# The last mixer of a four-layer chain: gate and upper projection by halves of columns, the first attention item ahead of the main loop, keys rotated later, compressed values copied later

## The reference, cut to what matters

```python
u = h @ w_in
q, kc, vc, ks, vs, kw, vw, gt, cf = jnp.split(u, offs, axis=-1)
...
# native_sparse_attention: three softmaxes over compressed, selected and window keys
q  = apply_rope(rms_norm(q, q_norm), cos, sin)
ks = apply_rope(rms_norm(k_slc, k_norm[0]), cos, sin)
kw = apply_rope(rms_norm(k_win, k_norm[1]), cos, sin)
kc = rms_norm(compress_blocks(to_bgtd(kc_tok), cmp_pos[0], cmp_w1[0], cmp_w2[0]), k_norm[2])
vc = compress_blocks(to_bgtd(v_cmp), cmp_pos[1], cmp_w1[1], cmp_w2[1])
...
# the conformer half, on the columns cf of the projection
a, b = jnp.split(cf, 2, axis=-1)
z = a * jax.nn.sigmoid(b)
z = causal_dwconv(z, conf_dw) + conf_dw_b
z = jax.nn.silu(layer_norm_2(z, conf_ln_g, conf_ln_b))
return jnp.concatenate([o_nsa, z], axis=-1) @ w_out
```

## Time and profile before

| what | value |
|---|---|
| median of 3 runs | 2250.28 us (2248.72 to 2250.85) |
| the profiled execution, its own time | 2246.99 us |
| span of the profile | 2245.2 us |
| PE busy | 2217.0 us, 99% of the span |
| DVE, ACT, POOL busy | 1632.4, 1197.9 and 129.6 us |
| last mixer, queries' projection to conformer | about 1929 to 2036 us in the span |

### The profile page before, as it was taken

How to read it: one execution, slowest core, us unless ns; L and a number is a source line. 1 busy time by engine, 2 the same in 40 slices (tenths; PEclk the granted TensorE clock), 3 DMA queues, 4 the chain that set the end, 5 groups by cost and what they waited for, 6 DMA issues and landing times.

```text
span 2245.2 us, 34615 instructions
## 1 busy us (share of the span) xinstructions
PE 2217.0 (99%) x14127; PEld 1903.4 (85%) x14127; DVE 1632.4 (73%) x2508; ACT 1197.9 (53%) x1896; POOL 129.6 (6%) x185
## 2 busy tenths in 40 slices
PE   9999999999999999999999999999999999989999
PEld 7888899878888888888898778888888888867887
DVE  5777768868676776768668867776877678666776
ACT  5555446645555545555356544655554655556653
POOL 2100010120000000000100110000000000420000
PEclk9999999999999999999999999999999999999999
DMA  7755564445556556655554446655655656643654
GB/s 243 226 188 192 188 222 122 146 142 188 190 187 192 187 186 209 192 190 195 196 181 140 140 143 210 196 188 170 215 174 171 213 188 190 200 134 117 197 176 150
DMA packets 284207, 408.17 MB, mean 182 GB/s; under 512 B 13828, under 2 KB 171072, under 8 KB 283792
## 3 DMA queue, kind: packets, MB, share of 16 engines
q1 hardware_dynamic: 276096, 380.84, 52.9%
q0 software_dynamic: 7808, 25.04, 3.8%
q10 hardware_dynamic: 144, 0.07, 0.0%
HBM read 403.98 MB, written 1.91 MB: 181 GB/s over the span
## 4 chain that ended last, share of the span: by engine, by line
PE 91%; DVE 5%; ACT 2%; DMA 1%; issue 1%; POOL 0%; SPq 0%; DVEq 0%; ACTq 0%
PE PS L575 24%; PE PS L506 13%; PE PS L513 12%; PE PS L507 12%; PE PS L574 11%; PE PS L472 3%; PE PS L473 2%; PE PS L474 2%; PE PS L577 2%; PE PS L558 1%; PE PS L556 1%; PE PS L557 1%; PE PS L492 1%; DVE WL L1391 1%; DVE QX L1698 1%; ACT WH L1007 1%
## 5 line engine op out<-in xcount | busy, mean ns | idle before, releaser
L1391 DVE TENSOR_TENSOR WL<-RW,WH 128x1024 fp32r<-128x1024 f32 (+2 forms) x678 | 806.6, 1223 | 160.4 <-ACT WH L1007 156.1
L575 PE MATMUL PS<-XT,WH 128*128 128x512 f32 x2368 | 808.0, 394 | 0.0
L1007 ACT ACTIVATE WH<-RW 128x1024 fp32r<-128x1024 f32 (+2 forms) x678 | 680.5, 1042 | 200.2 <-DMA RW<-in_w_in 40.2
L574 PE MATMUL PS<-XT,WL 128*128 128x256 f32 x2072 | 580.8, 280 | 0.0
L575 PEld LDWEIGHTS PS<-XT,WH 128*128 128x128 f32 x2368 | 425.1, 188 | 76.0
L574 PEld LDWEIGHTS PS<-XT,WL 128*128 128x128 f32 x2072 | 389.8, 188 | 13.4
L506 PE MATMUL PS<-WH,XT 128*128 128x512 f32 (+2 forms) x592 | 229.1, 391 | 1.4 <-DVE WL L1391 0.8
L507 PE MATMUL PS<-WL,XT 128*128 128x512 f32 (+2 forms) x592 | 221.4, 378 | 0.0
L506 PE MATMUL PS<-WH,HTH 128*128 128x512 f32 x488 | 192.7, 395 | 0.0
L507 PE MATMUL PS<-WL,HTH 128*128 128x512 f32 x488 | 191.5, 392 | 0.0
L513 PE MATMUL PS<-WH,XT 128*128 128x512 f32 (+2 forms) x592 | 173.5, 379 | 0.0
(11 more groups left out here) (519 smaller groups left out, 3282.7 us busy)
## 6 DMA issues: line engine op xcount, KB each, us to landing
RW<-in_w_ff_in SPq DMA_DIRECT2D x252, 512.0 KB, 4.4
RW<-in_w_ff_out SPq DMA_DIRECT2D x128, 512.0 KB, 4.4
RW<-in_w_in SPq DMA_DIRECT2D x56, 512.0 KB, 4.6
RW<-in_w_gate SPq DMA_DIRECT2D x48, 512.0 KB, 4.4
RW<-in_ffn_gate SPq DMA_DIRECT2D x44, 512.0 KB, 4.5
RW<-in_ffn_up SPq DMA_DIRECT2D x44, 512.0 KB, 4.6
RW<-in_ffn_down SPq DMA_DIRECT2D x44, 512.0 KB, 4.5
RW<-in_w_out SPq DMA_DIRECT2D x16, 512.0 KB, 4.8
```

What stands on the lines that cost most here:

```text
L574: self.e.matmul(k.PS[:, b.n, 0:T], wl, k.XTH[:, kt, :], start=False, stop=False)
L575: ins = self.e.matmul(k.PS[:, b.n, :], wh, k.XT[:, kt, :], start=kt == 0, stop=kt == 7)
L1007: self.e.activation(u.hi_out, raw, ACT.Copy).then_inc(*self.s["hi"].up(u.n))
L1391: self.e.tensor_tensor(u.lo_out, raw, u.hi_out.bitcast(F), ALU.subtract).then_inc(*self.s["lo"].up(u.n))
```

## The change

Five things are done in `mixer_odd` and its helpers.

1. The two rotations of the keys (and the copies on POOL behind the second) no longer stand ahead of the queries' projection; the first stands behind its fourth step, the second behind its eighth. `paired` stands behind the sixth and the seventh step.
2. Instead of the whole gate, the first half of the gate and the first half of the upper part are projected there, 256 columns wide, in pieces of 256 KB and eight steps as before. The main loop projects the second halves, gate first.
3. Item 0 is begun there: its scores behind the eighth step, `odd_max`, exponentials and `odd_scale` ahead of the main loop. In all items `odd_scale` stands straight behind the exponentials.
4. The copies of the compressed values to `VCB` are a function of their own, `cmp_values`, called behind item 0's exponentials; `odd_up` for the first half, `conv_out` and `conv_shift` are called before the main loop, and `conv_weights` ahead of the keys' `features`.
5. The delays of the generators change, item 1 begins with `compressed()`, and the `later` flag is gone.

```diff
     def cmp_out(self, b):
         k = self.k
         self.wait_ge("mm", b.full)
-        self.wait_ge("odd_g", "vcb0")
-        for i in range(4):
...
         kr = k.PS[:, b.n, 0:128].rearrange("p (g d) -> p g d", g=2)
...
+    def cmp_values(self, b):
+        k = self.k
+        self.wait_ge("odd_v", "kn0")
+        self.wait_ge("odd_g", "vcb0")
+        for i in range(4):
...
-        for t in range(2):
-            e.rotate("k", t, 8, 12)
         e.windows()
...
-        beside = [e.nothing] * 6 + [lambda: paired(0), lambda: paired(1)]
+        beside = [e.nothing, e.nothing, e.nothing, lambda: rotated_keys(0), e.nothing, lambda: paired(0),
+                  lambda: paired(1), lambda: rotated_keys(1)]
...
-            e.odd_scale(I)
             yield
...
+        beside = [lambda: e.rotate("q", 0, 0, 8), lambda: e.rotate("q", 1, 0, 8), hidden, cleared, hidden_turn,
+                  lambda: features("q", 0), lambda: (compressed_rows(), gated(0, gates)), lambda: next(items[0])]
+        for c0, bks in ((1816, gates), (1304, ups)):
+            for _ in self.cols(w, c0, 2, bks, self.x):
+                beside.pop(0)()
+        raised(0, ups)
+        features("q", 1)
+        next(items[0])
+        compressed_keys()
+        next(items[0])
+        e.cmp_values(*compressed_out)
+        self.drop(*compressed_out, ("odd_a", ("vcb", 3)), ("odd_v", "kn0"))
...
-            for half in range(2):
+            for c0, end in ((1816 + 256, gated), (1304 + 256, raised)):
...
-        gens = [(1, items[0]), (1, compressed()), (2, items[1]), (2, items[2]), (3, items[3]), (3, items[4]), (3, items[5]),
+        gens = [(0, items[0]), (1, compressed()), (0, items[1]), (2, items[2]), (3, items[3]), (3, items[4]), (3, items[5]),
                 (3, items[6]), (3, items[7])]
```

More of the change, by code:

```diff
@@ L459 @@
     conv_out = conv_shift = conv_weights = conv_taps4 = conv_sum = paired = odd_q = cmp_hidden = cmp_turn = cmp_out = features = keys_double = nothing
-    cmp_norm = cmp_keys = cmp_scores = cmp_probs = cmp_probs_turn = odd_scores = odd_max = odd_scale = odd_turn = odd_out = nothing
+    cmp_norm = cmp_values = cmp_keys = cmp_scores = cmp_probs = cmp_probs_turn = odd_scores = odd_max = odd_scale = odd_turn = odd_out = nothing
     conf_turn = conf_norm = conf_back = nothing
@@ L1300, in cmp_out @@
         self.wait_ge("mm", b.full)
-        self.wait_ge("odd_g", "vcb0")
-        for i in range(4):
-            r = slice(32 * i, 32 * i + 32)
-            self.e.activation(k.VCB[r, i], k.PS[r, b.n, 128:256].rearrange("p (g d) -> p g d", g=2),
-                              ACT.Copy).then_inc(*self.s["odd_a"].up(("vcb", i)))
         kr = k.PS[:, b.n, 0:128].rearrange("p (g d) -> p g d", g=2)
@@ L1311, in cmp_out @@
         self.e.activation(ms, ms, ACT.Sqrt, bias=k.eps[1e-6], scale=1.0 / 64).then_inc(*self.s["odd_a"].up("kroot"))
+    def cmp_values(self, b):
[3 more added lines that the diff above has]
+        for i in range(4):
+            r = slice(32 * i, 32 * i + 32)
+            self.e.activation(k.VCB[r, i], k.PS[r, b.n, 128:256].rearrange("p (g d) -> p g d", g=2),
+                              ACT.Copy).then_inc(*self.s["odd_a"].up(("vcb", i)))
     def cmp_keys(self, b):
@@ L3275, in mixer_odd, with rotated_keys @@
             load_w1()
-        e.keys_double()
+        def rotated_keys(t):
+            e.rotate("k", t, 8, 12)
+            if t:
+                e.keys_double()
         def paired(n):
@@ L3297, in hidden_turn @@
             self.drop(b, ("odd_a", ("gh", 1)))
+        compressed_out = []
         def compressed_rows():
@@ L3303, in compressed_rows @@
             e.prepare(ACT.Tanh)
-            self.drop(b, ("odd_a", "ksq"), ("odd_v", "kn0"))
+            compressed_out.append(b)
         def compressed_keys():
@@ L3320, in mixer_odd @@
         e.rotate_norms("q", 0, 8)
[L3324 to L3336, removed]
-        turned, done = set(), {0: [], 1: []}
[L3339 to L3355, removed]
+        turned, done = set(), {0: [], 1: []}
         def item(n, t, hs):
-            while any(ROOM[m] == ROOM[n] and m not in turned for m in range(n)) or ROOM[n] and not later["q1"]:
+            while any(ROOM[m] == ROOM[n] and m not in turned for m in range(n)) :
                 yield
@@ L3378, in item @@
                 e.prepare(ACT.Sqrt)
+            e.odd_scale(I)
             yield
-            e.odd_scale(I)
             yield
@@ L3393, in item @@
             yield
+            if n == 0:
+                yield
+                yield
+                yield
+                yield
             b = self.bank()
@@ L3401, in item, with gated, raised, cleared @@
             done[t].append(("turn_lo", I.id))
+            yield
+        items = [item(n, t, hs) for n, (t, hs) in enumerate(
+            [(0, [0, 2]), (0, [4, 6]), (0, [1, 3]), (0, [5, 7]), (1, [0, 1]), (1, [2, 3]), (1, [4, 5]), (1, [6, 7])])]
+        gates, ups = [self.bank(), self.bank()], [self.bank(), self.bank()]
+        def gated(half, bks):
+            for j in range(2):
+                e.odd_gate(2 * half + j, bks[j])
+                self.drop(bks[j], ("odd_a", ("sg", 2 * half + j)))
+        def raised(half, bks):
+            for j in range(2):
+                e.odd_up(2 * half + j, bks[j])
+                self.drop(bks[j], ("odd_v", ("zc", 2 * half + j)))
+            e.conv_out(half)
+            e.conv_shift(half)
+        def cleared():
+            e.clear_vcb()
+            for n in range(2):
+                e.conv_weights(n)
+            features("k", 0)
+            features("k", 1)
+        beside = [lambda: e.rotate("q", 0, 0, 8), lambda: e.rotate("q", 1, 0, 8), hidden, cleared, hidden_turn,
[10 more added lines that the diff above has]
+        self.drop(*compressed_out, ("odd_a", ("vcb", 3)), ("odd_v", "kn0"))
+        def compressed():
+            bks = [self.bank(), self.bank()]
+            e.cmp_scores(bks)
+            for b in bks:
+                self.drop(b, ("odd_v", "cs"))
+            yield
+            yield
+            e.cmp_probs()
+            yield
+            yield
+            b = self.bank()
+            e.cmp_probs_turn(b)
+            self.drop(b, ("odd_a", "ptc"))
             yield
@@ L3429, in upper @@
         def upper():
-            for half in range(2):
+            for c0, end in ((1816 + 256, gated), (1304 + 256, raised)):
                 bks = [self.bank(), self.bank()]
-                for n, _ in enumerate(self.cols(w, 1304 + 256 * half, 2, bks, self.x)):
+                for n, _ in enumerate(self.cols(w, c0, 2, bks, self.x)):
                     if n == 3:
[L3435 to L3439, removed]
+                        end(1, bks)
                     yield
         y = self.out_odd(Operand(k.OTH, k.OTL, lambda kt, t: done[t] if kt < 4 else [("turn_lo", ("conf", t))]))
-        items = [item(n, t, hs) for n, (t, hs) in enumerate(
-            [(0, [0, 2]), (0, [4, 6]), (0, [1, 3]), (0, [5, 7]), (1, [0, 1]), (1, [2, 3]), (1, [4, 5]), (1, [6, 7])])]
-        gens = [(1, items[0]), (1, compressed()), (2, items[1]), (2, items[2]), (3, items[3]), (3, items[4]), (3, items[5]),
+        gens = [(0, items[0]), (1, compressed()), (0, items[1]), (2, items[2]), (3, items[3]), (3, items[4]), (3, items[5]),
                 (3, items[6]), (3, items[7])]
-        up, conv, live, tick, ticks = upper(), convolve(), [], 0, 0
+        up, conv, live, tick = upper(), convolve(), [], 0
         outs = 0
@@ L3453, in mixer_odd @@
             tick += 1
-            ticks += 1
-            if ticks == 4:
-                later["q1"] = True
             live = [g for g in live if next(g, self) is not self]
```

## The result

The changed kernel takes 2253.07 us (median of 18 runs, 2250.79 to 2255.87), the kernel before 2249.96 in as many (2246.44 to 2254.76). The ratio is 1.0016 with a 95% interval of 1.0009 to 1.0022: slower by 3.1 us in the medians, and by 2 to 5 us, 0.1 to 0.2%, by the interval. The profiled executions differ by 3.80 us (2250.79 and 2246.99).

The account below looks back on a forecast made before the run. PE, busy 2217.0 of 2245.2 us, was taken as the bound, so only its waits and clock count. Terms -0.7 - 1.4 + 1.7 + 0 + 2.2 + 0 = +1.8 on the median 2250.28 gave 2252.1 us, range 2247.5 to 2256.5.

Parts of the forecast that it names:

- Keys rotated late: Gate's first steps: rotations moved into the queries' projection remove PE's wait for WL, -0.7 us.
- Values copied behind: Ahead of L897: moving the VCB copies off ACT's chain removes PE's whole wait for the compressed keys, -1.4 us.
- Item 0's softmax: Ahead of L943: chain of 9.4 us against 4.8 of PE cover, so 4.6 us of wait where 2.16 was.
- The waits behind it: After item 0's turn: 1.0 us before L920, where 2.25 was, and 0.5 before item 1's turn.
- Clock: Behind item 0's wait: the half-clock dip comes again at the same cost, 0, ends -1.7 and +1.7 us.
- Loop: Main loop: Z's wait of 0.8 goes, 0.7 given back for DVE's order, DG's wait stays; 0 in all.
- Tail: From the convolution's last step: L970 waits +1.0 us and L978 +1.2 as their cover moves; +2.2 in all.
- no dip: Rival, behind item 0's wait: the half clock doesn't come, -1.7 us, 2250.4; chance 0.18.
- The pieces land late: Rival, weight loads: 256 KB pieces landing after 8.6 us hold up the chain; +4 us, 2256; chance 0.15.

Follow-up runs that it names:

- x5: Changed kernel with the two key rotations back ahead of the queries' projection; 2255.53 us, 1.0024 of the kernel before.
- x9: Changed kernel run again unaltered, for a second profile; 2253.16 us, 1.0011 of the kernel before.
- x6: Changed kernel with the four copies to VCB back ahead of the squares; 2255.90 us, 1.0021 of the kernel before.
- x1: Changed kernel with 40 unread 128x128 transposes on PE ahead of item 0's turn; 2250.61 us, 1.0010 of the kernel before.
- x8: Kernel of x4 with 16 unread transposes ahead of compressed turn L920 and 14 ahead of item 1's turn; 2243.84 us, 0.9970 of the kernel before.
- x10: Kernel before the change with 18 unread transposes ahead of item 0's turn and 19 ahead of the compressed turn; 2251.35 us, 0.9999 of the kernel before.
- x7: Changed kernel with three of four products left out of each DG POOL makes from the third on; 2250.62 us, 1.0002 of the kernel before.
- x3: Changed kernel with item 1 two turns, item 2 one turn and so all later items later; 2247.22 us, 0.9992 of the kernel before.
- x4: Changed kernel with item 0's turn two turns later, compressed turn one, item 1 two, item 2 one; 2243.18 us, 0.9976 of the kernel before.
- x2: Changed kernel with only item 0's turn two loop turns later, its output where it was; 2250.91 us, 1.0010 of the kernel before.

## Why the prediction was right, and where it was not

The forecast was 2252.1, the median 2253.07; +1.8 us was summed, and the runs gave +3.1, the profiles +3.8. Most of the waits that it names came at their places, but its sum is half of what the mixer grew by, and the range, which reaches from 4.6 us below the forecast to 4.4 above, was wide enough to hold that. So the nearness of the median is in part luck. By its own steps:

- **Keys rotated late, -0.7**: right. The first gate step stands at 1940.76, 22.33 us into the mixer, for 23.25 before. x5 brings the wait back at 1.19; x9 shows that 0.33 can stay.
- **Values copied behind, -1.4**: right. L897 waits for nothing; x6 shows 1.18 for it.
- **Item 0's softmax, 4.6 of wait**: right, 4.52 (4.53 in x9). The chain was summed step by step from the earlier trace rows, and its cover from the earlier trace rows, and both hold: from the step behind L888, at 1961.14, to the turn it took 9.46 us for 9.4, of which PE worked 4.94 for 4.8. One reading beside it was short, without effect on the sum: before, a fourth step and item 1's scores stood between item 0's scores and its turn as well.
- **The waits behind it, 1.0 and 0.5**: right in size, and invisible in the changed kernel: x1 shows 1.14 and 0.42 once PE runs at full clock.
- **Clock, 0**: this step failed, a term of the sum that was mis-sized. I took the dip to come again at the same cost. It came, and lasted 10 us (13 in x9) instead of 3.4. From 1970.60 to the sixth projection triplet at 1980.33 PE took 9.73 us; for the same instructions x1 took 5.34 at full clock (1973.19 to 1978.53), so that the dip took 4.4 of PE's time for the 1.7 of before: +2.7. Of this 1.5 come back in the two waits that it hides. And time at half clock is no loss by itself: x8 and x10 gained no more than 0.5 us behind the next wait by taking it away, x1 about 2.5.
- **Loop, 0**: this step failed too. Z's wait (0.8) is gone as said. The wait for DG (0.62 before), which I took to stay, went as well. But the scaling of item 4 now runs beside POOL's DG, with 1.92 us of wait, where x7 has 0.64 and the kernel before none, and the second dip behind it; x7 prices the two at 2.1 together. I had given back 0.7 for DVE's order and not looked at what POOL does beside it.
- **Tail, +2.2**: right in mechanism, 0.96 and 0.91, sum 1.9; x3 takes both away.

With the measured sizes the sum is -0.9 (WL) - 1.4 (KCN) + 0.1 (4.52 for 2.16 and 2.25) + 2.7 (first dip) - 0.8 (Z) + 2.1 (item 4 and its dip) + 1.9 (tail) = +3.7. What it leaves out, the other 0.64 at item 4, 0.39 at item 3 and the 0.62 for DG that went, adds 0.4: +4.1, for the 3.81 by which the mixer grew.

Of the rivals, "no dip" fell with the window above. "The pieces land late" fell: the longest landing of RW was 6.8 us, for 8.6 in the earlier trace rows. DMA issues and landings after, in the stretches of the earlier trace rows:

```profile
RW<-in_w_in_odd SPq DMA_DIRECT2D x14, 256.0 KB, 3.5
...
DMA to landing us min/median/max: 2.7/3.9/6.8
```

## What to carry to other kernels

A softmax that is begun early is one chain over ACT and DVE: sum the chain and PE's cover from the same starting point, and start it early but ask for it late, as x4 does. A moved last item takes the cover of what follows it: name what stood behind it. And price a dip of the clock by what PE waits for next, not by its length.

## What the runs showed of the hardware that I had not expected

**DVE against POOL.** DVE's step on 128x4 elements took 0.17 us alone and 1.09 beside POOL's products of DG (2.71 in x5); two scalings took 1.29 alone and 4.01 in x1. POOL's eight products took 3.83, where the kernel before had 2.91 for them. The Trainium skill, page "SBUF — State Buffer", section "SBUF: two separate sides", says that a DVE step with two SBUF inputs and a GpSimd step that reads SBUF exclude each other, and that whichever starts first has the shared ports for the whole instruction. The traces agree that the two hold each other up; the scalings read two SBUF operands. Which of them goes first they do not show: in x5 the small step starts at 2009.25, 0.14 us ahead of POOL's products by its row, and is held until 2011.96, beside eight products of 2.91 in all, so over several of them. The kernel before had such a meeting too, without a wait of PE behind it: DVE's L2093 on 128x4 elements took 0.97 us at 2004.68, beside the products shown at 2003.07, and 0.17 at 1971.23. I had not looked at what runs on POOL when the scalings move.

**The clock.** It fell with PE idle for 4.5 us ahead (after, x3), for 1.9 (the second dip after, x4), and in x2 with only 0.33 of idle but L910 and L934 in a row. The length of a wait did not decide it: no dip followed 2.38 us before L920 in x2, 2.00 at item 4 in x9, or 1.94 for DG in x3, and one did follow 2.00 at item 4 in x2. A dip lasted 3.4 to 13.7 us. It lasted 10.2 us (after, x5, x6, x7) and 13.7 (x9) where L910 and L934 in a row stood behind the wait, 6.8 where L910 and projection steps did (x3), and 6.8 in x4 behind L920. What sets the length stays open.
